# Attention of a streaming encoder on one Trainium2 core: score units paired on the row halves of TensorE, fp32 transposes with high and low parts made from PSUM

## What is computed

```
q, k = rmsnorm(q, g_q), rmsnorm(k, g_k)            # per head, 64 wide; 8 query heads on 2 kv heads, per branch
logits = q . k * HEAD_DIM ** -0.5 + bias            # A: 256 best keys of the indexer, the rest masked; B: window
p = exp(logits - max);  out = (p @ v) / sum(p)      # B: a sink per head in max and sum
```

## Time and profile before

| | |
|---|---|
| median of 3 runs | 999.85 us (996.74 to 999.96) |
| the profiled execution | 1004.23 us, of it 1002.4 us span |
| TensorE, weight loads | 949.6 and 850.8 us busy (95% and 85%) |
| VectorE, ScalarE, GpSimd | 66%, 40%, 38% |
| granted clock, mean | 0.975 |
| attention, from the first scores to the output projection | 558.7 to 800.8 us |

### The profile page before, as it was taken

The page is one execution under the profiler, slowest core; times in us unless marked ns, Lnnn a source line. Parts: engine busy times, 40 slices in busy tenths (PEclk is TensorE's granted clock), DMA queues, the critical chain, the costliest instruction groups (busy, mean ns, idle before and its releaser), DMA issues.

```text
span 1002.4 us, 17554 instructions
## 1 busy us (share of the span) xinstructions
PE 949.6 (95%) x6431; PEld 850.8 (85%) x6431; DVE 660.6 (66%) x1378; ACT 398.4 (40%) x1178; POOL 377.9 (38%) x424
## 2 busy tenths in 40 slices
PE   4859999999999999999999898999999899999998
PEld 2558887888889999999999776788778599999998
DVE  6563366999999999999990476766665763331121
ACT  5664566454322322121211465666665622212100
POOL 0262124222243533121234376766630135536332
PEclk9989999999999999999999699999999899999999
DMA  9820013753461323232141834443325655524342
GB/s 323 310 76 22 25 39 111 218 170 106 146 203 65 112 81 109 76 115 70 62 145 52 258 107 129 119 120 109 106 62 143 198 160 178 154 77 152 109 132 74
DMA packets 110906, 125.85 MB, mean 126 GB/s; under 512 B 10969, under 2 KB 88153, under 8 KB 110698
## 3 DMA queue, kind: packets, MB, share of 16 engines
q1 hardware_dynamic: 100418, 113.77, 36.5%
q10 hardware_dynamic: 10408, 11.01, 3.6%
HBM read 94.96 MB, written 35.75 MB: 130 GB/s over the span
## 4 chain that ended last, share of the span: by engine, by line
PE 82%; issue 4%; POOL 4%; DMA 3%; DVE 3%; ACT 3%; SPq 1%; POOLq 0%; DVEq 0%; ACTq 0%
PE PS L1667 19%; PE PS L1669 19%; PE PS L1668 19%; PE PS L1945 6%; PE PS L1919 6%; PE PS L1855 4%; PE PS L1764 2%; PE PS L1878 2%; PE PS L1923 1%; POOL YO L1072 1%; PE PS L1728 1%; DMA XN<-in_x_prompt 1%; PE PS L1676 1%; DMA VB<-snat 1%; DMA URAW<-in_w_out 1%
## 5 line engine op out<-in xcount | busy, mean ns | idle before, releaser
L1667 PE MATMUL PS<-HH,WH 128*128 128x384 f32 (+1 forms) x576 | 188.8, 328 | 0.0
L1669 PE MATMUL PS<-HH,WL 128*128 128x384 f32 (+1 forms) x576 | 187.9, 326 | 0.0
L1668 PE MATMUL PS<-HL,WH 128*128 128x384 f32 (+1 forms) x576 | 187.7, 326 | 0.0
L1493 DVE MAX8 M<-SC 128x8 f32<-128x384 f32 (+3 forms) x210 | 174.8, 870 | 11.6 <-DVE SC L1498 11.0
L1498 DVE MATCH_REPLACE8 SC<-M,SC 128x384 f32<-128x384 f32 (+3 forms) x210 | 179.9, 864 | 0.0
L923 POOL TENSOR_TENSOR WL<-RAW,WH 128x512 fp32r<-128x512 f32 x72 | 93.9, 1309 | 159.2 <-ACT WH L1091 159.2
L1667 PEld LDWEIGHTS PS<-HH,WH 128*128 128x128 f32 x576 | 108.1, 188 | 3.7 <-issue 3.7
L1667 PE MATMUL PS<-WH,HH 128*128 128x512 f32 (+2 forms) x264 | 100.4, 380 | 8.7 <-DVE HL L1437 8.7
L1668 PEld LDWEIGHTS PS<-HL,WH 128*128 128x128 f32 x576 | 108.1, 188 | 0.0
L1669 PEld LDWEIGHTS PS<-HH,WL 128*128 128x128 f32 x576 | 108.1, 188 | 0.0
L1668 PE MATMUL PS<-WL,HH 128*128 128x512 f32 (+2 forms) x264 | 98.8, 374 | 0.0
(11 more groups left out here) (232 smaller groups left out, 1974.7 us busy)
## 6 DMA issues: line engine op xcount, KB each, us to landing
RAW<-in_w_all SPq DMA_DIRECT2D x72, 256.0 KB, 2.7
gz<-STG SPq DMA_DIRECT2D x48, 192.0 KB, 1.9
WADA<-in_w_ada SPq DMA_DIRECT2D x16, 512.0 KB, 12.0
snat<-STG SPq DMA_DIRECT2D x24, 256.0 KB, 2.0
QKV<-snat SPq DMA_DIRECT2D x8, 768.0 KB, 5.3
GT<-gz SPq DMA_DIRECT2D x32, 192.0 KB, 2.5
XN<-in_x_prompt SPq DMA_DIRECT2D x8, 512.0 KB, 6.1
btad<-bvd ACTq DMA_DIRECT2D x4, 1024.0 KB
```

Source lines behind the costliest of these rows:

```text
L1493: V.max(M8[0:r, a, :], w).then_inc(sel_step, 1)
L1667: T.matmul(out, wh, mh, start=first, stop=False)
L1668: T.matmul(out, wh, ml, start=False, stop=False)
L1669: return T.matmul(out, wl, mh, start=False, stop=last)
```

## The change

1. Pairs. Units s and s + 1 are made together at even s. The tiles of Q and K in SBUF now hold head dimension x kv head on the partitions: rows 0 to 63 belong to the even unit, 64 to 127 to the odd one. For each block there are three matmuls of 64 rows (qh kh, ql kh, qh kl) for each unit, in turns between the halves; the units' outputs lie in different banks. Units of up to 512 keys take one bank each, so there are two pairs of them in flight; longer ones take all four banks, and the next pair waits for the minima of both units.
2. Transposes. GpSimd normalises in place and orders the heads so that 128 columns hold one head of each kv head (XX, two buffers). TensorE transposes them in fp32, without parts: Q in two groups of four and K of both branches in one group of two for each tile, one transpose for each 128 cached keys. ScalarE makes the high part from PSUM, VectorE subtracts it from PSUM for the low part.
3. Order. Q and K of tiles 0 and 1 are transposed in the last pieces of the projection (six groups, before four); the others at steps 9, 11 and 13. QKV has one buffer. The bias table of tile 0 comes in two halves. The identity and mask of the sample have all 128 rows, with zeros.

```diff
+def scores_of(u):
+    b = 2 * (u % 2)
+    if unit_keys(u) > 512:
+        return PS[:, b:b + 2, :].rearrange("p b n -> p (b n)")
+    return bank(b + u // 2 % 2)
+def scores_free(u):
+    return u if max(unit_keys(u), unit_keys(u - 2) if u >= 2 else 0) > 512 else u - 2
...
         for tt in range(NT):
-            base = 16 * (tt - 1)
-            for j in range(4):
-                TP[base + 9 + j].append(("Q", tt, j))
-            for j in range(2):
-                TP[base + 13 + j].append(("K", tt, j))
+            for n, x in enumerate((("K", tt, 0), ("Q", tt, 0), ("Q", tt, 1))):
+                TP[16 * (tt - 1) + 9 + 2 * n if tt >= 2 else 3 * tt + n - 14].append(x)
...
-        EARLY_T = 4
+        EARLY_T = 6
+        EARLY_AT = {NP - 6: (0, 1), NP - 5: (2,), NP - 2: (3, 4), NP - 1: (5,)}
...
+        def split_high(act, x):
+            act.wait_ge(tr_pe, TIDX[x] + 1)
...
+            for high, _, src in split_parts(x):
+                last = nc.scalar.copy(high, src)
+            last.then_inc(split_hi, 1)
+        def split_low(dve, x):
+            dve.wait_ge(split_hi, EV[:TIDX[x] + 1].count("L"))
+            for high, low, src in split_parts(x):
+                last = nc.vector.tensor_tensor(low, src, high.bitcast(F32), ALU.subtract)
+            last.then_inc(tev_dve, 1)
...
 # GpSimd, one tile
-                    nc.gpsimd.tensor_tensor(XNB[0:r, :, :], XG[0:r, :, :],
-                                            RYQ[0:r, 20 * tt:20 * tt + 20].unsqueeze(2).broadcast_to([r, 20, HD]), ALU.mult).then_inc(xn4_ready, 1)
-                tt = prep(s, SPLIT_AT)
...
-                        nc.gpsimd.tensor_tensor(QS[0:r, 8 * br:8 * br + 8, 1, :], XNB[0:r, 10 * br:10 * br + 8, :],
-                                                QS[0:r, 8 * br:8 * br + 8, 0, :].bitcast(F32), ALU.subtract)
...
+                    nc.gpsimd.tensor_tensor(x, x, RYQ[0:r, 20 * tt:20 * tt + 20].unsqueeze(2).broadcast_to([r, 20, HD]), ALU.mult).then_inc(xn4_ready, 1)
...
 # TensorE, Q and K
-                    for b in range(4):
-                        last = T.transpose(out[:, 128 * b:128 * b + r].bitcast(F32R), src[b].rearrange("p a d -> p (a d)"), IDR[0:r, 0:r])
+                    first = [10 * x[2] + 2 * b for b in range(4)] if x[0] == "Q" else [8, 18]
+                    for b, h0 in enumerate(first):
+                        last = T.transpose(out[:, 128 * b:128 * b + r],
+                                           XX[x[1] % 2][0:r, h0:h0 + 2, :].rearrange("p a d -> p (a d)"), IDF[0:r, 0:r])
...
 # TensorE, scores
-                if 0 <= s < NU:
...
-                    if u >= 2:
-                        pe.wait_ge(min_done, u - 1)
...
-                        for part in range(2):
-                            last = T.matmul(out, q, keys[:, kv, part, k0 + b:k0 + b + m],
-                                            start=(part == 0), stop=(part == 1 and br == 1))
+                if 0 <= s < NU and s % 2 == 0:
...
+                    if scores_free(s) > 0:
+                        pe.wait_ge(min_done, scores_free(s))
...
+                        for n, (pq, pk) in enumerate(((0, 0), (1, 0), (0, 1))):
+                            for u in (s, s + 1):
+                                half = slice(HD * (u % 2), HD * (u % 2) + HD)
...
+                                last[u] = T.matmul(scores_of(u)[:, b:b + m], q, keys[half, pk, k0 + b:k0 + b + m],
+                                                   start=(n == 0), stop=(n == 2 and br == 1))
```

More of the change, by code:

```diff
@@ L304, in build_program @@
         zt_in = [sem(f"zt_in{i}") for i in range(2)]
-        qkv_in = [sem(f"qkv_in{i}") for i in range(2)]
+        qkv_in = sem("qkv_in")
         rms_ready = sem("rms_ready")
@@ L490, in build_program @@
         TIDX = {x: q for q, (_, x) in enumerate(TQ)}
[L491 to L492 removed]
+        EARLY_T = 6
+        EARLY_AT = {NP - 6: (0, 1), NP - 5: (2,), NP - 2: (3, 4), NP - 1: (5,)}
+        assert all(TQ[n][1][0] in "KQ" and TQ[n][1][1] == n // 3 for n in range(EARLY_T))
         PREP0 = {16 * (tt - 1): tt for tt in range(NT)}
[L494 to L495 removed]
+        LOAD_AT, NORM_AT, STORE_AT = -7, -5, 2
         RD_AT, FIN_AT = ({GEND[g] + d: g for g in range(2 * NT)} for d in (1, 4))
@@ L738, in _ @@
                         sp.wait_ge(stg2_out[i], 16 * ((NT + 1 - i) // 2))
-                    for tt in range(2):
-                        sp.dma_start(QKV[:, tt, :], snat[tcols(tt), :]).then_inc(qkv_in[tt], 16)
+                    sp.dma_start(QKV[:], snat[tcols(0), :]).then_inc(qkv_in, 16)
                     for dst, src in ((t["pa_v"], snat[0:SEQ, 640:768]), (t["sa_v"], snat[SEQ:TOK, 640:768]),
@@ new lines, in _ @@
+                    pool.wait_ge(qkv_in, 16 * (tt + 1))
+                    if tt >= 2:
+                        pool.wait_ge(k_out, 16 * k_stores(tt - 2))
+                        pool.wait_ge(tr_pe, TIDX[("Q", tt - 2, 1)] + 1)
+                    for g, (c0, h0) in enumerate(((0, 0), (512, 8), (768, 10), (1280, 18))):
+                        if g % 2:
+                            last = nc.gpsimd.tensor_tensor(x[:, h0:h0 + 2, :], QKV[0:r, c0:c0 + 128].rearrange("p (h d) -> p h d", h=2),
+                                                           GAM[0:r, g:g + 1, :].broadcast_to([r, 2, HD]), ALU.mult)
+                        else:
+                            nc.gpsimd.tensor_tensor(x[:, h0:h0 + 8, :].rearrange("p (j k) d -> p k j d", k=2),
+                                                    QKV[0:r, c0:c0 + 512].rearrange("p (k j d) -> p k j d", k=2, j=4),
+                                                    GAM[0:r, g:g + 1, :].unsqueeze(1).broadcast_to([r, 2, 4, HD]), ALU.mult)
@@ L1238, in _ @@
                     bias_table(j)
-                if c == NCH - 1 and j == 9:
-                    t_evac(act, nc.scalar.copy, TQ[1][1], tev_act)
+                for n in EARLY_AT.get(p, ()):
+                    split_high(act, TQ[n][1])
             def attention_high(q):
@@ L1914, in _ @@
-                    kv = h // 2 if tt == SAMPLE else h // 4
+                        keys, k0 = (KTBS, 0) if tt == SAMPLE else (KT[:, 1], 128 * max(tt - 1, 0))
+                    last = {}
                     for b in range(0, nk, 512):
                         m = min(512, nk - b)
-                        out = PS[:, 2 * (u % 2) + b // 512, 0:m]
-                        for part in range(2):
-                            last = T.matmul(out, q, keys[:, kv, part, k0 + b:k0 + b + m],
-                                            start=(part == 0), stop=(part == 1 and br == 1))
-                        if br == 0:
-                            r = rows_of(tt)
-                            last = T.matmul(out, ident, MASK[0:r, MOFF[tt] + b:MOFF[tt] + b + m], start=False, stop=True)
@@ L1925, in _ @@
+                    for u in (s, s + 1):
+                        if br == 0:
+                            ident = IDP[:].rearrange("p a n -> p (a n)") if tt == SAMPLE else IDB[:]
+                            for b in range(0, nk, 512):
+                                m = min(512, nk - b)
+                                last[u] = T.matmul(scores_of(u)[:, b:b + m], ident, MASK[:, MOFF[tt] + b:MOFF[tt] + b + m], start=False, stop=True)
+                        last[u].then_inc(qk_pe, 1)
                 for x in TP[s]:
```

205 lines of the change are left out of this document (80 added, 125 removed).

## The result

The changed kernel takes **1011.3 us** (median of 4 runs, 1010.8 to 1013.73), the kernel before 999.85 (996.74 to 999.96): ratio 1.0127, 95% interval [1.0101, 1.0153], so it is slower by 1.3%. Later groups timed the kernel before 9 to 21 times each and had medians of 1001.2 to 1002.0; against these the slowdown is 0.9 to 1.0%. The forecast was 1000.5, no change. The profiled execution took 1011.71, its span is 1009.9. That is 7.5 us over the profiled execution of the kernel before, which lay 4.4 above its own median.

The account below looks back on a forecast made before the run. TensorE, busy 95% of the span, was taken to bound the kernel by its work and its waits before PV. Walk -1.2, projection transposes +0.4, new waits +1.5: +0.7 us, 1000.5 as median; 80% range 984 to 1013.

Parts of the forecast that it names:

- rival of late loads: Scores: a load waits for the stream of its own half, 0.32 a round at 512 keys; 1010 us, chance 8%.
- Step 1: Scores: streams of the halves overlap, loads do not; 0.64 a block, +0.1 for 256-key pairs, -0.66 for 1024-key pairs.
- rival with 27%: Scores: loads of the two halves overlap too, 0.32 a block at 256 keys or fewer; -13, 987 us, chance 27%.
- step 3: Attention iterations: scores no longer cover the 1.37 between P transposes and PV; short iterations +0.4, first of a tile +0.8.
- Step 2: Q, K and cache transposes: 141 fewer at 0.107, about 15 us of TensorE's work, counting only where they covered no latency.
- the walk: Attention summed iteration by iteration: tiles 0 to 7 -0.5, +2.0, -2.1, +1.2, +1.4, +0.1, -0.4, -1.9, sample -1.0; sum -1.2.
- tile 1: Attention tile of 256 keys: forecast to get 2.0 us longer.
- Step 5: New waits on ScalarE's high and VectorE's low parts: 0.2 us on about 7 iterations, +1.5.
- waits of scores for minima, called covered: Long units: a pair waits for both of VectorE's minima; taken as 0, or +0.3 in 18 pairs if not.
- tile 7: Attention tile of 1024 keys: forecast to get 1.9 us shorter.
- sample tile: Sample tile of the attention: forecast -1.0, as its masks no longer change the shape.
- Step 4: Edits of one answer: four more transposes in the projection, +0.4; K transposes, GpSimd work and the single QKV buffer 0.

Follow-up runs that it names:

- experiment 3: Changed kernel with the pairing undone: each unit scored alone in its own step with its half-height matmuls; 1061.6 us, ratio 1.0592.
- experiment 1: Changed kernel with P transposes, and those of denominators, issued ahead of the pair's scores, and VectorE copying before its minimum; 1007.1 us, ratio 1.0051.
- Experiment 4: Changed kernel with six small bf16 filler matmuls between P transposes and the wait for their copies, in steps up to 39; 1009.0 us, ratio 1.0072.
- experiment 7: Changed kernel with only the P transposes ahead of the pair's scores, those of denominators and cache staying behind; 1005.7 us, ratio 1.0036.
- experiment 2: Changed kernel with all score matmuls of a pair's first unit issued ahead of those of the second; 1012.4 us, ratio 1.0113.
- experiment 11: Unpaired kernel (each unit scored alone) with six full-height bf16 filler matmuls ahead of each PV up to step 39; 1054.8 us, ratio 1.0527.

## Why the forecast of no change was wrong

1011.3 lies inside the stated range of 984 to 1013, near its end, and that is luck. The range reached so far up for the rival of late loads (1010), which the rows refute: a round of 512 keys costs 0.233 us there, not 0.32. The forecast's own spread of some 4 us around 1000.5 does not reach it.

**Step 1, scores: wrong in its mechanism, and too dear in its sum.** Loads and streams of the two halves both overlap, as the rival with 27% said. The price of a block is then one half's streams and 0.19, where I had 0.12 for the change of shape. A pair of 256 keys costs 0.55 (I had 0.76; before 0.66), one of 1024 keys with masks 2.46 (I had 2.28, with 1.40 for the twelve matmuls that take 1.59; before 2.94). With 32 pairs of 256 keys and four of 1024 this comes to some 6 us less than I priced, an estimate from these differences; I had the lengths in between right by 0.2 or better. Part of it went into the longer wait of step 3. The Trainium skill ("TensorEngine Tiling (Array Packing)", Key Properties) says that different tiles load and multiply in parallel; experiment 3 agrees, with 1.59 for one half and 1.59 for both. That rival's 987 did not come for the reason of step 3.

**Step 2, transposes: right in the count.** There are 95 where there were 236, 141 fewer. TensorE's busy time in the attention fell by 12.6 us (without the missing records) although more of it ran at the lower clock; what of this is transposes and what scores was not separated. It gained nothing where they had covered a latency.

**Step 3, the cover: right, and it decides.** I had 1.37 between P transposes and PV; at the start of a tile it is 1.37, at its end 1.44 to 1.97. A short iteration was forecast at 2.72 and measures 2.66 in the last of tile 6, 0.55 + 1.52 + 0.59. The first of tile 4, forecast at 3.9, takes 3.70, because its scores take 1.74 and not 1.94. Tiles 2 to 5 came within 0.6 us each of the walk. Putting P transposes ahead of the scores gave back some 5 us, a part of it by an earlier rise of the clock (experiment 1).

**Its tile 1: the largest miss, 5.0 of 10.9 us.** This is the step that failed most. I worked out what the tile loses at one clock, and not what its new idle time does to the clock, which stands in no term for that tile. TensorE's weight loads between 570 and 590 fell from 14.71 to 9.90 us of busy time, and the rise of the clock moved from 581 to 595. Experiment 4 confirms it: with the wait filled the rise comes at 583, and tiles 0 and 1 are within 1 us of the walk.

**Step 5, new waits: too small, and one term was set to 0.** The waits of scores for minima, called covered, appear in tile 7, as 0.35 and 0.28:
```profile
751.51 1.65 PE L1912 MATMUL PS<-KT,QT 64*128 64x512 f32 x12 [0.35 <-DVE NM L1588]
753.10 1.04 PE L1919 MATMUL PS<-MASK,IDB 128*128 128x512 bf16 x4
...
756.77 1.66 PE L1912 MATMUL PS<-KT,QT 64*128 64x512 f32 x12 [0.28 <-DVE NM L1588]
```
With four pairs that cost 0.18 more each than priced this is 1.35, about the 1.5 by which that tile missed; but its four pairs of 256 keys cost 0.84 less than priced, so something of that size is not accounted for. A P copy that queues behind a split costs up to 0.6 beyond the bare latency (1.97 against 1.37 at 603.75). In the sample tile (2.2 off) I overlooked what is queued ahead of a copy that has lost its cover: the 3.35 us reciprocal.
```profile
788.88 3.35 DVE L1613 RECIPROCAL RDX<-DEN 128x512 f32<-128x512 f32 x1
...
793.51 1.12 PE L1941 MATMUL PS<-PT,VB 128*64 128x128 f32 x8 [3.61 <-DVE PT L598]
```
**Step 4: small, with the wrong sign.** I had +0.4. The first score comes 1.2 us earlier, and the stage from the output projection on takes 200.6 us (before 201.6, with 3.6 at the lower clock).

The misses of all tiles add to 10.9 us: the walk's -1.2 becomes +9.7 (the +1.5 of step 5 was put on top of the walk). With the 2.2 won outside the stage this is the 7.5 by which the profiled executions differ. How much of it is the clock and how much the copies is known only roughly: 2 to 5 us from experiment 4 for the clock, some 5 from experiments 1 and 7 for the copies; the two overlap, since those runs also raised the clock earlier. Tile 6's miss of 1.5 I did not follow, and how much of the rest is a loop of minimum, exp, transposes and copy that now bounds an iteration was not separated.

## What to carry to other kernels

Before putting two units side by side, look at what the second one stood between: this stage saved some 13 us of array time and lost 22 to waiting, because the work that moved was what hid a copy. Where the array's clock has fallen, ask also what new idle time does to the clock: here the rise came 14 us later, and work put into the wait brought it forward again. When a copy loses its cover, everything queued ahead of it on its engine lands on the path, so list that queue, the rare long operation too; and when a copy is moved to another queue, look at who takes over the one after it.

## What the runs showed of the hardware

- Matmuls on the two row halves overlap also when three in a row are issued to the same half (experiment 2: 1.66 us by the rows for twelve of 512 columns in either order, starting in six rounds of two), so interleaving by hand isn't needed over such a distance.
- A group of half-height matmuls costs 0.19 us once, and each then 0.01 to 0.02 more than its columns at 2.4 GHz (experiment 3 and the changed kernel: 0.55, 0.72, 0.89, 1.59 for 256, 384, 512 and 1024 keys).
- TensorE busy with mostly half-height matmuls did not get its clock back over 34 of 34 us busy at the 1.2 GHz level in experiment 11 and 60 of 60 in experiment 3. Full-height fillers brought the rise forward in all three kernels in which they were tried; whether by their rows or by their mere number is not told apart.
